# Attention of a two-part network on one core: two heads share an output tile, and the probabilities are normalised before their transpose

## The reference

```
def attention_blocks(q, k, v):            # 16 heads, dk = 96, dv = 64
    s = einsum('bqhrd,bkhd->bhrqk', qi, k) * scale
    p = softmax(s, axis=-1)
    return einsum('bhrqk,bkhe->bqhre', p, v)

q = (rms_norm(cq) @ w_uq)                 # per head 64 plain and 32 rotary columns
kv = (rms_norm(ckv) @ w_ukv)              # per head 64 key and 64 value columns
q_rope, kr = axial_rope(q_rope), axial_rope(kr)   # image tokens only, kr shared by all heads
y = (o * silu(gate)) @ w_out
```

## Time and profile before

| quantity | value |
|---|---|
| median of three runs | 2364.95 us |
| the profiled execution | 2368.89 us, span 2367.1 us |
| PE, DVE, ACT, POOL busy | 87%, 48%, 35%, 29% of the span |
| attention loop, 229 to 594 us | PE 355.1 busy of 365 us, DVE 237.6, ACT 112.7, POOL 19.0 |
| mean granted PE clock | 0.928 of full speed |

### The profile page before, as it was taken

One profiled execution on the slowest core, in us unless ns is written; L12 is line 12 of the kernel. 1 busy time (PEld: TensorE's weight loads), 2 busy tenths in 40 slices (PEclk: granted clock), 3 DMA queues, 4 the chain that ended last, 5 costly groups with the idle time before them and its releaser, 6 DMA issues.

```text
span 2367.1 us, 27756 instructions
## 1 busy us (share of the span) xinstructions
PE 2066.5 (87%) x10852; PEld 1683.4 (71%) x10852; DVE 1143.4 (48%) x1717; ACT 819.1 (35%) x1113; POOL 689.7 (29%) x304
## 2 busy tenths in 40 slices
PE   4899999999969789778484879999979997999997
PEld 3787878778858677667273658788758875878875
DVE  3331666666457577576699243313332524331332
ACT  3253232332233444543331243324332324332332
POOL 1121000000312232232135424444333542444442
PEclk9799999999979799889697989999989998999998
DMA  7111111111111101112120213332222321322321
GB/s 277 36 54 45 63 54 63 55 63 63 63 47 39 33 28 45 36 29 92 34 69 18 80 63 98 89 98 90 89 80 81 99 89 57 103 85 92 99 82 52
DMA packets 46545, 167.72 MB, mean 71 GB/s; under 512 B 5424, under 2 KB 5552, under 8 KB 46160
## 3 DMA queue, kind: packets, MB, share of 16 engines
q1 hardware_dynamic: 44496, 159.93, 21.1%
q10 hardware_dynamic: 1920, 6.02, 0.7%
HBM read 163.83 MB, written 2.10 MB: 70 GB/s over the span
## 4 chain that ended last, share of the span: by engine, by line
PE 72%; DVE 20%; ACT 5%; issue 2%; DMA 1%; ACTq 0%; POOL 0%; DVEq 0%
PE ps L430 19%; PE ps L431 19%; PE ps L432 19%; PE ps L527 4%; PE ps L537 3%; DVE ex L1116 2%; PE ps L558 2%; DVE hf L1116 2%; DVE acc L1116 2%; DVE sq L1116 2%; DVE Alo L1116 1%; DVE hf L1122 1%; ACT sq L792 1%; DVE tmp L1116 1%; PE ps L464 1%
## 5 line engine op out<-in xcount | busy, mean ns | idle before, releaser
L1100 POOL TENSOR_TENSOR wlo<-raw,whi 128x1024 fp32r<-128x1024 f32 x253 | 616.5, 2449 | 1550.2 <-ACT whi L775 1550.2
L430 PE MATMUL ps<-Ahi,whi 128*128 128x512 f32 (+1 forms) x1328 | 529.8, 399 | 43.9 <-issue 23.5
L431 PE MATMUL ps<-Alo,whi 128*128 128x512 f32 (+1 forms) x1328 | 522.8, 394 | 0.0
L432 PE MATMUL ps<-Ahi,wlo 128*128 128x512 f32 (+1 forms) x1328 | 517.0, 389 | 0.0
L775 ACT ACTIVATE whi<-raw 128x1024 fp32r<-128x1024 f32 x253 | 259.9, 1055 | 701.2 <-PE ps L432 680.2
L430 PEld LDWEIGHTS ps<-Ahi,whi 128*128 128x128 f32 x1328 | 257.6, 194 | 121.8 <-issue 38.9
L432 PEld LDWEIGHTS ps<-Ahi,wlo 128*128 128x128 f32 x1328 | 257.3, 194 | 54.1
L431 PEld LDWEIGHTS ps<-Alo,whi 128*128 128x128 f32 x1328 | 258.3, 194 | 47.8 <-issue 0.2
L1122 DVE SCALAR_TENSOR_TENSOR cv<-ps,vec,cv 128x511 f32<-128x511 f32 (+1 forms) x176 | 131.9, 750 | 320.6 <-ACT cv L792 315.9
L430 PE MATMUL ps<-Fhi,whi 128*128 128x512 f32 x416 | 167.3, 402 | 12.9 <-DVE Flo L1116 12.8
L431 PE MATMUL ps<-Flo,whi 128*128 128x512 f32 x416 | 165.5, 398 | 0.0
(11 more groups left out here) (231 smaller groups left out, 3227.3 us busy)
## 6 DMA issues: line engine op xcount, KB each, us to landing
raw<-in_units SPq DMA_DIRECT2D x301, 512.0 KB, 3.6
X<-in_xT ACTq DMA_DIRECT2D x1, 2048.0 KB, 12.8
out_xT<-X SPq DMA_DIRECT2D x8, 256.0 KB, 2.0
CX<-in_ctxT ACTq DMA_DIRECT2D x1, 1024.0 KB, 15.1
masks<-in_masks ACTq DMA_DIRECT2D x1, 512.0 KB, 3.5
gmw<-in_gmw ACTq DMA_DIRECT2D x1, 384.0 KB, 2.8
bs<-in_bs ACTq DMA_DIRECT2D x1, 384.0 KB, 3.8
vec<-in_vec ACTq DMA_DIRECT2D x1, 312.5 KB, 4.5
```

The costliest lines, as they stand in the source:

```text
L430: nc.tensor.matmul(out, sh, mh, start=first, stop=False)
L431: nc.tensor.matmul(out, sh, ml, start=False, stop=False)
L432: return nc.tensor.matmul(out, sl, mh, start=False, stop=last)
L1100: nc.gpsimd.tensor_tensor(wlo[:, s % CONV, :], raw[:, plan.unit_at[("split", s)] % RAW, :], whi[:, s % CONV, :].bitcast(fp32), ALU.subtrac ...
```

## The change

- Units are ordered by pairs of heads: for each block of queries first the even head, then the odd one. The even head keeps its 96 rows, the odd head has its rows in the order rotary-swapped, rotary, plain, and its score contracts over 128 rows, of which 32 rows of K are zero (cleared once by POOL).
- K is projected for two heads in one tile, with 64 columns each. Q is still one tile for each head. ACT copies all 128 rows of Q to SBUF (`q_raw`), and DVE `q_rope` has three products, all from SBUF. K is copied in two halves. The first Q, Q and K tiles and the tile of `kr` stand ahead of V.
- DVE passes the reciprocal to ACT (`rc`), and ACT `normalise` multiplies `Pr` by it in place. `Pr` has three buffers. In body `u` ACT does `softmax(u + 2)` and then `normalise(u + 1)`.
- `out` is done once for two units: V is stationary with 64 columns, the transposed probabilities are the moving operand with 128 columns, and the two heads go to partitions 0 to 63 and 64 to 127 of one tile. DVE multiplies this 128x128 result with the gate, in place in `gate0`.
- The transposes of `O` and the split behind them go. Once per pair ACT copies the high part (`pair_high`) and POOL takes the low part (`pair_low`).
- PSUM tiles of the loop have fixed places: scores 0 and 1, `out` and odd transposes 2, even transposes, Q, K, `ada` and `ada_t` 3.

```diff
@@ Plan @@
+        queries0(0)
+        queries0(1)
+        keys0(0)
         vt = [("uv", k, m) for k in range(2) for m in range(8)]
...
+            tile(("S", u), [("p", u + 1)], slots=[u % 2])
+            tile(("O", p, q), [("og", TN * p + q + 1)], slots=[2])
...
@@ tensor: the loop @@
+            for u in range(NU):
+                p, q, i = u // (2 * TN), u // 2 % TN, u % 2
                 if u + 2 < NU:
                     score(u + 2)
+                if i == 0 and u:
+                    out(*divmod(u // 2 - 1, TN))
                 ps = tile(("PT", u))
-                pe.wait_ge(sem("p"), u + 1)
+                pe.wait_ge(sem("pn"), u + 1)
...
+                if i:
+                    if q < 2 and p + 1 < PAIRS:
+                        queries0(2 * p + 2 + q)
+                    if q == 2 and p + 1 < PAIRS:
+                        keys0(p + 1)
+                    if q in (2, 4):
+                        ada(*more[2 * p + (q - 2) // 2])
+                    if q in (3, 5):
+                        ada_t(*more[2 * p + (q - 3) // 2])
@@ tensor: out @@
+                for n, t in enumerate(keys):
+                    for i in range(2):
+                        h = 2 * p + i
+                        last = nc.tensor.matmul(ps[64 * i:64 * i + 64, 0:P], V[:, t, h * HV:(h + 1) * HV],
+                                                PT[:, i, n * P:(n + 1) * P], start=n == 0, stop=n == len(keys) - 1)
@@ scalar @@
+            def normalise(u):
+                ac.wait_ge(sem("rc"), u + 1)
+                n = P * len(unit_keys(UNITS[u][1]))
+                act(Pr[:, u % 3, 0:n], Pr[:, u % 3, 0:n], ACT.Copy, None, small[:, 2, u % 8:u % 8 + 1], "pn")
+            def pair_high(p):
+                ac.wait_ge(sem("og"), TN * p + TN)
+                act(Ohi[:, p, :], gate0[:, p, :], ACT.Copy, sem_name="oh")
...
                 if u + 2 < NU:
                     softmax(u + 2)
+                if u + 1 < NU:
+                    normalise(u + 1)
+                if i:
+                    if q < 2 and p + 1 < PAIRS:
+                        queries0(2 * p + 2 + q)
+                    if q == 2 and p + 1 < PAIRS:
+                        keys0(p + 1)
+                    if q == 1 and p:
+                        pair_high(p - 1)
+            pair_high(PAIRS - 1)
@@ gpsimd @@
+            def pair_low(p):
+                po.wait_ge(sem("oh"), p + 1)
+                nc.gpsimd.tensor_tensor(Olo[:, p, :], gate0[:, p, :], Ohi[:, p, :].bitcast(fp32),
+                                        ALU.subtract).then_inc(sem("ol"), 1)
@@ vector: the loop @@
+                if u + 1 < NU:
+                    inverse(u + 1)
                 if u + 2 < NU:
                     row_max(u + 2)
+                if i == 0:
+                    if u:
+                        out(*divmod(u // 2 - 1, TN))
+                n = P * len(unit_keys(q))
                 ps = psum(("PT", u))
+                do(nc.vector.tensor_copy(PT[:, i, 0:n], ps[:, 0:n]), ("pta", "ptb")[i])
+                if i:
+                    if q < 2 and p + 1 < PAIRS:
+                        q_rope(2 * p + 2 + q)
```

More of the change, by code:

```diff
@@ L65 @@
 RAT = {n: 8 * i for i, n in enumerate(RESID)}
-UNITS = [(h, q) for h in range(H) for q in range(TN)]
+PAIRS = H // 2
+UNITS = [(2 * p + i, q) for p in range(PAIRS) for q in range(TN) for i in range(2)]
 NU = len(UNITS)
@@ L94, in __init__, with tile @@
         self.last = {}
-        n = 0
-        def tile(key, free, weights=(), again=None):
-            self.index[key] = len(self.free)
+        self.slot, self.before, self.in_slot, self.turn = [], [], {}, 0
+        def tile(key, free, weights=(), again=None, slots=None):
+            self.index[key] = n = len(self.free)
             self.free.append(free)
+            slot = (slots or range(BANKS2))[self.turn % len(slots or range(BANKS2))]
+            self.turn += 1
+            self.slot.append(slot)
+            self.before.append(self.in_slot.get(slot))
+            self.in_slot[slot] = n
             start = len(self.split)
@@ L161, in __init__ @@
         for u in range(NU):
[L162 to L167, removed]
+            p, q, i = u // (2 * TN), u // 2 % TN, u % 2
             if u + 2 < NU:
                 score(u + 2)
[L170 to L175, removed]
+            if i == 0 and u:
+                out(*divmod(u // 2 - 1, TN))
+            tile(("PT", u), [(("pta", "ptb")[i], u // 2 + 1)], slots=[3 - i])
+            if i:
+                if q < 2 and p + 1 < PAIRS:
+                    queries0(2 * p + 2 + q, [3])
+                if q == 2 and p + 1 < PAIRS:
+                    keys0(p + 1, [3])
+                if q in (2, 4):
+                    ada(*more[2 * p + (q - 2) // 2], slots=[3])
+                if q in (3, 5):
+                    ada_t(*more[2 * p + (q - 3) // 2], slots=[3])
+        out(PAIRS - 1, TN - 1)
         for m in range(8):
@@ L407, in tile @@
                 at[0] += 1
[L408 to L409 removed]
+                if plan.before[n] is not None:
+                    for name, value in plan.free[plan.before[n]]:
                         pe.wait_ge(sem(name), value)
[L411 removed]
+                return PS[plan.slot[n]]
             def done(last):
@@ L546, in _ @@
             for u in range(NU):
[L547 to L552, removed]
+                p, q, i = u // (2 * TN), u // 2 % TN, u % 2
                 if u + 2 < NU:
                     score(u + 2)
+                if i == 0 and u:
+                    out(*divmod(u // 2 - 1, TN))
                 ps = tile(("PT", u))
[L556 to L558 removed]
+                pe.wait_ge(sem("pn"), u + 1)
+                for n in range(len(unit_keys(q))):
+                    last = nc.tensor.transpose(ps[:, n * P:(n + 1) * P], Pr[:, u % 3, n * P:(n + 1) * P], ident[:, :])
                 done(last)
[L560 to L567 removed]
+                if i:
[3 more added lines that the diff above has]
+                        keys0(p + 1)
+                    if q in (2, 4):
+                        ada(*more[2 * p + (q - 2) // 2])
+                    if q in (3, 5):
+                        ada_t(*more[2 * p + (q - 3) // 2])
+            out(PAIRS - 1, TN - 1)
+            for m in range(8):
+                ps = tile(("l0", m))
+                for k in range(KD):
+                    pe.wait_ge(sem("ol"), k + 1)
+                    w = tuple(weights(("l0", m), k))
+                    for c0, c1 in BOTH:
+                        last = product(ps[:, c0:c1], w, (Ohi[:, k, c0:c1], Olo[:, k, c0:c1]), k == 0, k == KD - 1)
                 done(last)
[L569 to L571 removed]
             norm("n1")
@@ L1254, in _, with out @@
+            def out(p, q):
+                ps = psum(("O", p, q))
+                g = gate0[:, p, q * P:(q + 1) * P]
+                ve.wait_ge(sem("gate0"), p + 1)
+                tt(g, ps[:, 0:P], g, MUL, "og")
             more = [(0, j) for j in range(8, 12)] + [(1, j) for j in range(12)]
             q_rope(0)
+            q_rope(1)
             row_max(0)
             row_max(1)
+            inverse(0)
             for u in range(NU):
-                if u % TN == 1 and u // TN + 1 < H:
-                    q_rope(u // TN + 1)
@@ L1280, in _ @@
-            flush()
+                do(nc.vector.tensor_copy(PT[:, i, 0:n], ps[:, 0:n]), ("pta", "ptb")[i])
+                if i:
+                    if q < 2 and p + 1 < PAIRS:
+                        q_rope(2 * p + 2 + q)
+                    if q in (2, 4):
+                        ada(*more[2 * p + (q - 2) // 2])
+                    if q in (3, 5):
+                        ada_t(*more[2 * p + (q - 3) // 2])
+            out(PAIRS - 1, TN - 1)
+            scales(1)
             def resid(key, m, gate=None, n_sem="resid"):
```

197 lines of the change are left out of this document (102 added, 95 removed).

## The result

The changed kernel takes 2370.98 us, the median of 18 runs (2364.05 to 2375.33), beside 2365.16 us for the kernel before in 18 runs (2361.23 to 2368.47). The ratio is 1.002, with a 95% interval of 1.0012 to 1.0028. The forecast was 2353: it was wrong in its sign. The profiled execution took 2368.15 us with a span of 2366.4, 2.8 us under its median.

The account below looks back on a forecast made before the run. The loop was taken as bound by PE. From a span of 2367.1 us, 6.8 (loop), 0.3 (ahead) and 5.1 (behind) gave 2354.9, or 2356.7 executed and a median of 2353 us; range 2315 to 2379.

Parts of the forecast that it names:

- PE's work: Attention loop: PE's work for a pair of heads falls from 44.5 to 37.1 us, through K and `out`.
- 0.17 for changing over: Part of the 1.45 us price of a full pair's `out`: 0.17 us added for PE's change of mode.
- The chain: Score to `out` through the queues of ACT and DVE: stalls of 8.9 us a pair, which takes 46.0 us.
- behind the first Q: Bodies 2 and 3 of a pair: PE stalls 1.9 us, until `normalise` of unit 3 ends.
- behind the second with POOL beside it: Bodies 4 and 5: the same 1.9 us stall, plus 1.1 in six pairs from `pair_low` beside `q_rope`'s third product.
- before `ada`: Behind K in bodies 4 and 5: `ada`, in the same PSUM place, waits 1.9 us for both K copies.
- body 1: Transposes of unit 1 wait 1.1 us, with ACT making the pair's weight block before softmax(2).
- small ones that did not come: Waits in a pair: 0.3 us at the transposes of 0, 0.1 and 0.2 in the bodies from 6 on.
- The loop in sum: Start, eight pairs and their waits: 363.4 us against 370.2, so 6.8 us less.
- rival 3: Clock falls in the loop's new 2 us gaps, 3 us a pair: +24, 2377 us; chance 0.12.
- Ahead of the loop: Before the first score: one more Q costs 3.15 us, the 3.49 wait for Q goes; sum -0.3 us.
- Behind the loop: Last `out` to the end of the first `l0` tile: 17.3 us against 22.4, so -5.1 us.

Follow-up runs that it names:

- e5: Changed kernel with both heads of `out` in the same 64 columns of the array (odd heads' output not the reference's): 2394.48 us, ratio 1.0124.
- e1: Changed kernel with POOL's clearing of the 32 rows of K moved to the start of POOL's list: 2362.69 us, ratio 0.9983 to the kernel before.
- e11: Changed kernel without the three `q_rope` products for all heads but the first two (output not the reference's): 2345.00 us, ratio 0.9915.
- e2: Changed kernel with the K projection directly behind the second Q of a pair instead of ahead of `ada`: 2333.87 us, ratio 0.9872.
- e6: Changed kernel with K cleared early, K projected behind the second Q and `pair_high` two blocks later: 2328.16 us, ratio 0.9841.
- e8: e6 plus `normalise` before the next softmax on ACT and the reciprocal ahead of `q_rope` on DVE: 2316.70 us, ratio 0.9790.
- e9: e8 plus weight blocks of the loop and the first of `l0` up to 12 tiles ahead instead of 7: 2295.22 us, ratio 0.9711.

## Why the prediction was wrong

**PE's work: `out` right, the sum short.** A full `out` was put at 1.45 us and takes 1.46 (341.79 to 343.25 in the timeline), its load 0.055. But an ordinary pair of 47.7 us holds 8.7 us of waits of PE, so its work is 39.0 us, not 37.1 (the terms as given add up to 37.2). No single term is far off: a full score that another operand's work follows takes 1.4 to 1.46 us and not 1.32, full transposes 0.7 and not 0.66, K 2.3 and not 2.1.

The two rules of the Trainium skill that the prediction weighed come out as the trace before showed it. Against the first ("TensorE: Matmul & The Clock Gate", Part 3, "The mechanism": a weight load overlaps a running matmul only when the row groups differ), the loads hide here with all rows in use: 24 loads and products take 1.46 us in two column halves, and 2.77 in one (e5), where load and product in turn would take 3.9. The second ("TensorEngine Tiling", "Key Properties": a change of mode drains the engine) is not tested: the price with 0.17 for changing over fits, which does not prove it.

**The chain: right in its mechanism, its size in part by luck.** Stalls forecast and found in an ordinary pair, us: behind the first Q 1.9 and 1.7, behind the second with POOL beside it 3.0 and 3.2, before `ada` 1.9 and 1.8, body 1 1.1 and 0.8, `out` of body 8 0.6 and 0.6, transposes of body 11 0.9 and 0.6. With small ones that did not come (0.3, 0.1 and 0.2) the forecast had 10.0 us of waits, and 8.7 are there. That the pair comes out near, 47.1 against 47.7, is luck: 1.9 us too little work and 1.3 too much waiting nearly cancel. Normalise takes 0.94, not 0.85.

**The loop in sum: mis-sized, the second step that failed.** 374.1 us (230.15 to the end of the last `out` at 604.25) against 363.4. Of the 10.7, four ordinary pairs give 2.6 and two with a fall of the clock 4.2; the first pair, also with a fall, 2.5; the start 0.7 (the half clock behind the first wait, see e1) and the last pair 0.7. The fall was rival 3, priced at 3 us a pair in all pairs from the 6.8 us at half speed behind the loop; it came in three pairs and lasts 3.4 us (0.79 over 8 us), so it cost about 1.5. The loop before was put at 370.2 us; its last `out` ends at 593.57 and not at 594.0, so it was 369.8, and the change made the loop 4.3 us longer where 6.8 less were forecast. The last `out` before and after:

```profile
592.94 0.63 PE L537 MATMUL ps<-V,PT 128*128 128x64 f32 x4 [0.28 <-DVE PT L1269]
```

```profile
603.59 0.66 PE L567 MATMUL ps<-hf,V 128*64 128x128 f32 x8
```

**Ahead of the loop: the first step that failed.** The text had -0.3, "the six V tiles cover `q_rope`". They do. But the clearing of K by POOL, in the change's description and in no term of the sum, stands behind a weight block in POOL's list. The first score started at 230.15, 6.7 us later than I had it, and 6.2 of these are the wait for it behind the last V copy. Moving that one instruction (e1) gives back 8.3 us in the medians, of which the traces show 7.5: the 6.2 and the 1.3 of the half clock behind the wait.

**Behind the loop: right, a little better.** -6.9 against -5.1 from the end of the last `out` to the first result, with the 594.0 of the prediction for the end before (10.3 us late at 604.25, 3.4 late at 620.02 against 616.62); from 593.57 it is -7.3. PE starts 5.7 us behind `out` (5.9 forecast).

Together: 6.7 + 10.7 - 1.8 = 15.6 us above the forecast at that point. The seven other `l0` tiles then come at 8.21 instead of 8.43 us, 1.5 in all, and the last result of `l0` is at 677.50 against 675.59, 1.9 us late. That is what the change costs in the two traces. The medians differ by 5.8, and the executions of the changed kernel scatter more (11 us against 7). What makes the other 4 us was not settled. The stages behind are unchanged code, and between the two traces they drift by a few us to either side.

The choice in the prediction that decided the sign was to count gains of 12 us in a sum where 58 us of saved work stood against 51 us of waits. A term of 7 us that is left out, and 10 us on the loop, is more than that.

## What to carry to other kernels

When work is taken from the engine that bounds a software pipeline, walk one period through every in-order queue: a step queued behind the wait for a later unit (normalise behind the next softmax, maximum and reciprocal behind a filler) gives the gain back without any engine being busy. Then list every instruction that the change adds to each queue, one-time ones too, with what stands ahead of it; here one clear cost as much as the loop was forecast to gain. Fillers belong where their consumers are covered by PE work, K behind Q, and once the waits are gone the next late thing is a supply that was timed for the slower loop, here the weight blocks.

## What the runs showed of the hardware

Two fp32 products of 64 stationary and 128 moving columns run beside each other in the two column halves, all 128 rows in use: 24 in 1.46 us, and 2.77 when they share the columns. A DVE product with both operands in SBUF that meets a POOL subtraction ends about 0.5 us after POOL is done (355.66 and 355.12): 2.18 us instead of 0.68. The granted clock fell for 3.4 us behind waits of PE no longer than 2.2 us, in every pair of e11, and not at all in the loops of e2, e6, e8 and e9, from the third score on, whose pairs lack the wait before `ada`. The `l0` tiles of the same shape take 8.21 us from `Ohi`, `Olo` and 8.43 from `Ahi`, `Alo`; why was not tried.
